# Splitting the compressed branch's softmax and row sums into two halves of the query blocks

## The reference

```
logits = einsum(q, ck) * ATTN_SCALE             # 1024 queries x 32 compressed keys, per head
logits = where(cend <= qpos, logits, -inf)      # mask by block end
e      = exp(logits - max(logits))              # m = 0 where a row has no key
p_cmp  = e / where(sum(e) > 0, sum(e), 1)
o_cmp  = einsum(p_cmp, cv)
mix    = sum over branches of sigmoid(gl) * o * silu(z)
y      = x + gate * (mix @ w_out)
```

## Time and profile before

| what | value |
|---|---|
| time, median of 3 runs | 1786.0 us (1785.25 to 1787.79) |
| profiled execution | 1782.46 us |
| its span in the trace | 1780.7 us |
| PE busy | 1623.2 us, 91% |
| DVE busy | 911.3 us, 51% |
| ACT busy | 599.7 us, 34% |
| POOL busy | 501.1 us, 28% |

### The profile page before, as it was taken

One profiled execution on the slowest core, in us unless ns is written; L12 is line 12 of the kernel. 1 busy time (PEld: TensorE's weight loads), 2 busy tenths in 40 slices (PEclk: granted clock), 3 DMA queues, 4 the chain that ended last, 5 costly groups with the idle time before them and its releaser, 6 DMA issues.

```text
span 1780.7 us, 31773 instructions
## 1 busy us (share of the span) xinstructions
PE 1623.2 (91%) x11976; PEld 1453.3 (82%) x11976; DVE 911.3 (51%) x2356; ACT 599.7 (34%) x1315; POOL 501.1 (28%) x304
## 2 busy tenths in 40 slices
PE   3899999997896988799999999999999999998887
PEld 1688888886795987788888889888898888976777
DVE  1445455455325143455655556556555565577355
ACT  2523333343004042224434344343443434443112
POOL 0131322116531234281111111111102111049462
PEclk9899999999898988899999999999999999999998
DMA  9123232223321144310111131111110111133822
GB/s 351 50 99 125 92 111 101 101 102 132 119 95 72 54 165 126 86 36 22 39 37 34 31 77 40 60 34 28 34 40 13 34 28 34 28 98 110 270 72 107
DMA packets 81586, 146.20 MB, mean 82 GB/s; under 512 B 19059, under 2 KB 52883, under 8 KB 81267
## 3 DMA queue, kind: packets, MB, share of 16 engines
q1 hardware_dynamic: 68202, 129.69, 22.5%
q10 hardware_dynamic: 10288, 8.46, 1.5%
q0 software_dynamic: 2944, 6.04, 1.2%
HBM read 130.01 MB, written 19.35 MB: 84 GB/s over the span
## 4 chain that ended last, share of the span: by engine, by line
PE 81%; DVE 7%; ACT 4%; issue 3%; DMA 3%; SPq 1%; POOL 0%; ACTq 0%; DVEq 0%
PE PS L935 15%; PE PS L937 14%; PE PS L936 14%; PE PS L1182 9%; PE PS L1195 9%; PE PS L1162 4%; PE PS L1163 4%; PE PS L1274 2%; PE PS L1172 1%; PE PS L1191 1%; PE PS L1127 1%; PE PS L966 1%; ACT XT L1383 1%; ACT HT_r L1386 1%; DMA KD<-w_bo 1%
## 5 line engine op out<-in xcount | busy, mean ns | idle before, releaser
L935 PE MATMUL PS<-HT_r,WR_r 128*128 128x344 f32 x1368 | 461.7, 337 | 29.2 <-DVE XT_r L1650 24.4
L937 PE MATMUL PS<-HT_r,WR_r 128*128 128x344 f32 x1368 | 445.0, 325 | 0.0
L936 PE MATMUL PS<-XT_r,WR_r 128*128 128x344 f32 x1368 | 444.7, 325 | 0.0
L625 POOL TENSOR_TENSOR WR_r<-WR,ONE 128x1024 fp32r<-128x1024 f32 x65 | 125.8, 1936 | 1093.4 <-DMA WR<-w_b 645.6
L1462 ACT ACTIVATE PB<-PB,NM 128x257 f32<-128x257 f32 (+9 forms) x384 | 248.9, 650 | 176.2 <-DVE NM L1841 176.0
L935 PEld LDWEIGHTS PS<-HT_r,WR_r 128*128 128x128 f32 x1368 | 265.7, 194 | 34.7 <-issue 26.5
L936 PEld LDWEIGHTS PS<-XT_r,WR_r 128*128 128x128 f32 x1368 | 265.2, 194 | 0.0
L937 PEld LDWEIGHTS PS<-HT_r,WR_r 128*128 128x128 f32 x1368 | 264.3, 193 | 0.0
L1182 PE MATMUL PS<-CST,PB 128*128 128x128 f32 (+1 forms) x1360 | 227.0, 286 | 1.8 <-ACT PB L1458 1.5
L1854 DVE COPY PT<-PS 128x256 f32<-128x256 f32 (+2 forms) x192 | 121.6, 633 | 198.7 <-PE PS L1182 198.1
L1195 PE MATMUL PS<-PT,VT 128*64 128x128 f32 x2592 | 202.9, 284 | 5.2 <-DVE SS L1894 1.8
(11 more groups left out here) (289 smaller groups left out, 2342.8 us busy)
## 6 DMA issues: line engine op xcount, KB each, us to landing
WR<-w_ada SPq DMA_DIRECT2D x64, 512.0 KB, 5.1
WR<-w_b SPq DMA_DIRECT2D x32, 512.0 KB, 3.4
WR<-w_a SPq DMA_DIRECT2D x17, 512.0 KB, 5.6
STR<-scratch SPq DMA_DIRECT2D x128, 48.0 KB, 1.9
KD<-w_bo SPq DMA_DIRECT2D x9, 512.0 KB, 3.5
XT<-x SPq DMA_DIRECT2D x8, 516.0 KB, 15.1
HT<-x SPq DMA_DIRECT2D x8, 516.0 KB, 4.6
x_mid<-HT SPq DMA_DIRECT2D x8, 516.0 KB, 6.2
```

The lines of the kernel that those rows point to most:

```text
L625: pool.tensor_tensor(high_r, raw, ONE[:, 0:1].unsqueeze(2).to_broadcast([P, NC, P]), ALU.mult).then_inc(sem("w_split"), 1)
L935: pe.matmul(out, hw[:, k, :], high, start=(k == 0), stop=False)
L936: pe.matmul(out, hw[:, k, :], low, start=False, stop=False)
L937: return pe.matmul(out, lw[:, k, :], high, start=False, stop=(k == NC - 1))
```

## The change

The compressed `sm` is run twice, on four query blocks each: all five instructions of it stand twice, on half the columns. The first half counts up a new semaphore `c_sm`, the second the old one. The exponential becomes two, on 256 columns each; the first waits for `c_sm` and counts up a new `c_ex`. The transposes of the first four blocks and `rg` of the first half wait for `c_ex`. The row sums and their clamp stand in both `rg` now, each on its own half.

```diff
# PE, step "tr"
-                            pe.wait_ge(sem(ph + "_ex"), un["parts"][-1]["x"] + 1)
+                            pe.wait_ge(*((sem("c_ex"), un["it"] + 1) if un["b"] == "cmp" and x["ends"]["half"] == 0
+                                         else (sem(ph + "_ex"), un["parts"][-1]["x"] + 1)))
# ACT, step "ex"
-                            p_ = PB[:, sl, un["at"]:un["at"] + un["keys"]]
-                            act.activation(p_, p_, ACT.Exp).then_inc(sem(ph + "_ex"), 1)
+                            n = un["keys"] // 2
+                            for half in range(2):
+                                act.wait_ge(*((sem("c_sm"), un["it"] + 1), (sem(ph + "_sm"), x["x"] + 1))[half])
+                                p_ = PB[:, sl, un["at"] + n * half:un["at"] + n * half + n]
+                                act.activation(p_, p_, ACT.Exp).then_inc(sem(("c", ph)[half] + "_ex"), 1)
# DVE, step "sm"
-                            for i in range(2):
-                                ins = dve.scalar_tensor_tensor(x4[:, :, i, :], scores[:, :, i, :], -SCALE, mask, ALU.mult, ALU.add)
-                            step(ins)
-                            step(dve.tensor_reduce(NM[:, 4, :], x3, AX, ALU.min))
-                            step(dve.tensor_scalar(NM[:, 4, :], NM[:, 4, :], BIG / 10, None, ALU.min))
-                            dve.scalar_tensor_tensor(x3, x3, -1.0, NM[:, 4, :].unsqueeze(2).to_broadcast([P, 2 * QB, NCB]),
-                                                     ALU.mult, ALU.add).then_inc(sem(ph + "_sm"), 1)
+                            for half in range(2):
+                                n, q0 = L // 2, QB // 2 * half
...
+                                for i in range(2):
+                                    ins = dve.scalar_tensor_tensor(x4[:, :, i, :], scores[:, :, i, :], -SCALE, mask, ALU.mult, ALU.add)
+                                step(ins)
+                                step(dve.tensor_reduce(nm, x3, AX, ALU.min))
+                                step(dve.tensor_scalar(nm, nm, BIG / 10, None, ALU.min))
+                                dve.scalar_tensor_tensor(x3, x3, -1.0, nm.unsqueeze(2).to_broadcast([P, QB, NCB]),
+                                                         ALU.mult, ALU.add).then_inc(sem(("c", ph)[half] + "_sm"), 1)
# DVE, step "rg"
-                        if b == "cmp" and half == 0:
-                            p4 = PB[:, un["slot"], un["at"]:un["at"] + un["keys"]].rearrange("p (q s c) -> p q s c", q=QB, s=2)
-                            step(dve.tensor_reduce(den, p4, AX, ALU.add))
-                            step(dve.tensor_scalar(den, den, 1.0 / BIG, None, ALU.max))
+                        if b == "cmp":
+                            n = un["keys"] // 2
+                            p4 = PB[:, un["slot"], un["at"] + n * half:un["at"] + n * half + n].rearrange("p (q s c) -> p q s c", q=QB // 2, s=2)
+                            own = den[:, 4 * half:4 * half + 4, :]
+                            step(dve.tensor_reduce(own, p4, AX, ALU.add))
+                            step(dve.tensor_scalar(own, own, 1.0 / BIG, None, ALU.max))
```

More of the change, by code:

```diff
@@ L1454, in pairs @@
                         sl = un["slot"] + s
-                        act.wait_ge(sem(ph + "_sm"), x["x"] + 1)
-                        if un["b"] == "cmp":
-                            p_ = PB[:, sl, un["at"]:un["at"] + un["keys"]]
-                            act.activation(p_, p_, ACT.Exp).then_inc(sem(ph + "_ex"), 1)
[L1459 to L1463, removed]
+                        if un["b"] == "cmp":
+                            n = un["keys"] // 2
[3 more added lines that the diff above has]
+                                act.activation(p_, p_, ACT.Exp).then_inc(sem(("c", ph)[half] + "_ex"), 1)
+                            continue
+                        act.wait_ge(sem(ph + "_sm"), x["x"] + 1)
+                        at = 1 if ph == "a" else 0
+                        out = PB[:, sl, un["at"] - at:un["at"] + un["keys"]]
+                        act.activation(out, PB[:, sl, 0:at + un["keys"]], ACT.Exp, scale=-1.0, bias=NM[:, sl, 0:1],
+                                       accum_out=DEN[:, BR[un["b"]], s, un["qb"]:un["qb"] + 1]).then_inc(sem(ph + "_ex"), 1)
                     elif what == "ev" and x["c"] % 2 == 0:
@@ L1818, in pairs @@
-                            step(ins)
-                            step(dve.tensor_reduce(NM[:, 4, :], x3, AX, ALU.min))
-                            step(dve.tensor_scalar(NM[:, 4, :], NM[:, 4, :], BIG / 10, None, ALU.min))
-                            dve.scalar_tensor_tensor(x3, x3, -1.0, NM[:, 4, :].unsqueeze(2).to_broadcast([P, 2 * QB, NCB]),
-                                                     ALU.mult, ALU.add).then_inc(sem(ph + "_sm"), 1)
+                            for half in range(2):
+                                n, q0 = L // 2, QB // 2 * half
+                                xx = PB[:, sl, un["at"] + n * half:un["at"] + n * half + n]
+                                x4 = xx.rearrange("p (q s c) -> p q s c", q=QB // 2, s=2)
+                                x3 = xx.rearrange("p (q c) -> p q c", c=NCB)
+                                mask = CST[:, C_CM + q0 * NCB:C_CM + (q0 + QB // 2) * NCB].rearrange("p (q c) -> p q c", q=QB // 2)
+                                scores = PS[:, 1, n * half:n * half + n].rearrange("p (q s c) -> p q s c", q=QB // 2, s=2)
+                                nm = NM[:, 4, QB * half:QB * half + QB]
+                                for i in range(2):
[5 more added lines that the diff above has]
+                                                         ALU.mult, ALU.add).then_inc(sem(("c", ph)[half] + "_sm"), 1)
@@ L1857, in pairs @@
                         un = [u for u in pl["units"] if u["it"] == it and u["b"] == b and u["qb"] in (None, 4 * half + 3)][0]
-                        dve.wait_ge(sem(ph + "_ex"), un["parts"][-1]["x"] + 1)
+                        dve.wait_ge(*((sem("c_ex"), it + 1) if b == "cmp" and half == 0 else (sem(ph + "_ex"), un["parts"][-1]["x"] + 1)))
                         den = DEN[:, BR[b], :, :].rearrange("p s q -> p q s")
-                        if b == "cmp" and half == 0:
-                            p4 = PB[:, un["slot"], un["at"]:un["at"] + un["keys"]].rearrange("p (q s c) -> p q s c", q=QB, s=2)
-                            step(dve.tensor_reduce(den, p4, AX, ALU.add))
-                            step(dve.tensor_scalar(den, den, 1.0 / BIG, None, ALU.max))
+                        if b == "cmp":
[4 more added lines that the diff above has]
+                            step(dve.tensor_scalar(own, own, 1.0 / BIG, None, ALU.max))
                         rg = RG[:, :, :]
```

## The result

The changed kernel takes 1790.41 us (median of 20 runs, 1787.97 to 1793.60), the kernel before 1785.05 us (median of 20, 1781.53 to 1789.58). The ratio is 1.0026, 95% interval 1.0019 to 1.0034: slower by 3.4 to 6.1 us. In a later comparison on another chip it was 1.0040 (1.0026 to 1.0053). The forecast was 1791.8 us, slower by 5.8.

A forecast was written before the change was run, and what follows sets the result against it. PE, 81% of the span, was taken to wait for DVE's chain; pair terms 3 x 0.93 + 0.6 - 2 x 0.23 + 0.44 + 2.4 = 5.8 us gave 1788.3, plus 3.5 for the median: 1791.8 us, range 1787.0 to 1797.5.

The forecast's parts named there:

- The place: PE's wait before the first half's transposes for DVE's reciprocal-gate product: 24.5 us in nine waits, growing to about 30.
- The instruction term: Compressed softmax and first row sums on DVE: two halves add 0.71 us, shorter sums save 0.27; net +0.44 per pair.
- The waits for POOL: DVE clamps and two-SBUF-input operations wait for a running POOL instruction; with this blocking the sum is 5.8 us, without 3.5.
- The formula of pair 1: DVE's chain in pair 1: POOL begins at 1.95 us, the chain ends at 8.84 instead of 7.91, +0.93.
- the tie: Pair 4: POOL's start at 1.17 us against the first half's subtraction at 1.18; DVE first -0.23, POOL first +1.5.
- the middle: Pair 4: +0.6 us, taken between -0.23 if DVE goes first and +1.5 if POOL does.
- The early exponential and the semaphores: Half one's exponential and transposes come earlier; worth nothing, as PE waited 1.5 us for the exponential in the whole layer.
- The second `rg`: Sums and clamp added there, 0.66 us, are covered by the fill with 4 us left; uncovered, 5.3 us.
- The clock: Rival, chance 0.20: pair 7's stall of 2.1 us also drops PE's clock, 3.1 us more, 1794.9 us.
- The faster rival: Halves slip past POOL in the compressed softmax chain: -6.6 us, 1779.4 us if it never met POOL; chance 0.07.

The follow-up runs named there:

- The first half early: Changed kernel with POOL's splits held back and the first half of the compressed softmax moved before DVE's last copy of the previous unit: 1746.77 us, ratio 0.9789.
- POOL held back: POOL's weight splits falling into the compressed softmax wait until the first `rg` is done: kernel before 1755.37 us, again 1751.94; changed kernel 1767.95 us.

## Why the prediction was right

*The place.* It named PE's one wait per pair for the end of DVE's chain. That wait grew by 5.8 us in the profile (24.5 to 30.3), and the experiments that shortened or lengthened the chain in all pairs moved the time the same way. The first half early, which shortened PE's stall in seven pairs and lengthened it in pair 0, did not move it.

*The instruction term, 0.44 us per pair.* Measured 0.45 in pair 7 (7.01 less 6.56), and 0.44 in seven pairs with POOL held back.

*The waits for POOL.* The formula of pair 1, which ends the chain 6.89 us after POOL's start, gives 9.29 for the start at 2.40 that pair 1 had; 9.26 were measured. It gives 8.71 and 8.58 for pairs 2 and 3; 8.70 and 8.56 were measured. So the mechanism holds, and the terms hang on POOL's start. Pairs 3 and 5 gained 0.30 and 0.37 where 0.23 was counted, pair 4 fell on DVE's side of the tie (-0.23 where the middle, +0.6, was counted), pair 0 lost 2.41 where 2.4 was counted. Pair 1 was mis-sized, at +0.93 where its chain grew by 1.35, and so was pair 6: counted like pair 1, its chain grew by 0.43, because POOL started at 1.38 and not at 1.88. Where POOL starts differs from run to run by some tenths, and the sum of the eight terms hung on that more than the text allowed.

*Luck in the sum.* The eight chains grew by 4.5 us together (64.0 to 68.6 in the table), where the terms sum to 5.8. PE's eight stalls grew by 5.85 us, more than the chains, because PE reached the wait earlier behind the softmax's start in pairs 0, 3, 4 and 5 (in pair 3 at 5.04 us instead of 5.49), which is PE waiting longer for the same end and costs no time. That 5.8 us was counted and 5.8 measured at this wait is in part luck.

*The early exponential and the semaphores* were called worth nothing; nothing can be measured. *The second `rg`* was called hidden; in this kernel it is.

*The clock* was kept out of the sum, as a rival at 0.20 that needs pair 7 to drop. In the profile after it did, in part: 7.96 us from the first transposes to the second, at a mean granted clock of 0.79, where 6.44 stood before (in the second profile of the changed kernel it did not drop: 6.44), while pair 4 had 7.93 instead of 9.49 and pair 1 10.68 instead of 9.54. Over the eight pairs these stretches sum to 74.05 us after and 72.82 before. So this term was small here, 1.2 us, because the stalls before were long enough to drop the clock already, and not because the clock does not matter: with POOL held back the same 0.44 us per pair, with 1.1 in pair 0, came with some 11 us more that the lower clock took.

*The faster rival* would have needed POOL out of the chain. That is what holding it back does, and there the changed kernel is 17 us faster than before, but slower than the unchanged one on the same base.

## What to carry to other kernels

Before splitting a step for overlap, find what the other engine waits for next: an earlier first half is worth nothing if a later step of the same chain is waited for anyway, and each half pays the fixed part of every instruction again (284 ns for 128 columns against 420 for 256 in the earlier trace rows). When a tiny instruction is sometimes ten times its usual length, lay the other engines' timelines beside it: here POOL's splits could wait until the chain was done without PE waiting for one of them, and holding them back by one more wait of POOL in each of pairs 0 to 6 was worth five to six times what the change under study cost. A short stall of PE is also priced by what its clock does afterwards, so shortening one can pay more than its length: here 4.2 us of stall went with some 11 us that the lower clock took.

## What the runs showed of the hardware that was not expected

The drop of PE's clock is not tied to a stall of a certain length. A stall of 1.66 us, which had none in pair 7 before, was followed by a stretch at the lower clock in five of seven pairs of the kernel before with POOL held back (pair 2: 9.51 us of work instead of 6.44, the others 7.9 to 8.0) and in two of seven in its second profile. One of 2.10 us was followed by a long one in three of seven pairs and by a short one in a fourth, and one of 1.39 us by a short one in one of seven (7.93 us). Stalls of 0.85 us were followed by none in seven, and those of before, 2.97 to 3.52 us in pairs 0 to 6, by one each time. In between the length does not decide: what else does was not found.

A DVE instruction of 8 numbers per partition (0.17 us) took 1.82 us beside POOL, and which of two instructions 0.03 us apart came first decided some 1.6 us of the chain (9.92 against 8.36).
